# A feed-forward down projection as Strassen block products, seven in place of eight, in a one-core decoder trunk

## The reference, cut to what matters

```python
def swiglu(h, w_gate, w_up, w_down):
    return (jax.nn.silu(h @ w_gate) * (h @ w_up)) @ w_down      # h 256x1024, inner width 2816
# layer 0
x = x + swiglu(rms_norm(x, ffn_norm[j]), ffn_w_gate[j], ffn_w_up[j], ffn_w_down[j])
# layer 1
x = x + pooling_mixer(rms_norm(x, pool_norm[j]), pool_w[j], pool_scale[j])
x = x + moe_swiglu(rms_norm(x, moe_norm[j]), moe_w_router[j], moe_w_gate[j], moe_w_up[j], moe_w_down[j])
```

## Time and profile before

| | us |
|---|---|
| three runs, median (lowest to highest) | 1188.87 (1187.67 to 1188.97) |
| the profiled execution | 1187.06 |
| its span, first to last instruction | 1185.2 |
| TensorE busy in the span | 1155.3 |
| VectorE busy | 190.6 |
| ScalarE busy | 129.3 |
| GpSimd busy | 15.3 |
| bytes moved by DMA | 402.93 MB, mean 340 GB/s |

### The profile page before, as it was taken

One profiled execution on the slowest core, in us unless ns is written; L12 is line 12 of the kernel. 1 busy time (PEld: TensorE's weight loads), 2 busy tenths in 40 slices (PEclk: granted clock), 3 DMA queues, 4 the chain that ended last, 5 costly groups with the idle time before them and its releaser, 6 DMA issues.

```text
span 1185.2 us, 15075 instructions
## 1 busy us (share of the span) xinstructions
PE 1155.3 (97%) x6514; PEld 557.3 (47%) x6515; DVE 190.6 (16%) x382; ACT 129.3 (11%) x280; POOL 15.3 (1%) x52
## 2 busy tenths in 40 slices
PE   8999999999999999999999999999999999999995
PEld 7647888874474342344333335333333533333331
DVE  2642000000042120110121011011101102110102
ACT  1352000010031110000111000011100001010002
POOL 1300000000000000000000000000000000000000
PEclk9999999999999999999999999999999999999998
DMA  8434046536655799999999999999999999999992
GB/s 303 196 123 197 2 176 251 233 140 245 247 232 235 322 402 364 417 431 429 429 431 430 392 429 429 431 431 427 426 433 431 427 430 429 433 427 427 432 430 98
DMA packets 18838, 402.93 MB, mean 340 GB/s; under 512 B 3264, under 2 KB 3264, under 8 KB 4032
## 3 DMA queue, kind: packets, MB, share of 16 engines
q1 hardware_dynamic: 18752, 401.67, 80.7%
HBM read 400.61 MB, written 1.05 MB: 339 GB/s over the span
## 4 chain that ended last, share of the span: by engine, by line
PE 89%; DMA 7%; DVE 2%; ACT 1%; issue 0%; SPq 0%; DVEq 0%; ACTq 0%
PE bank L1321 31%; PE bank L1413 13%; PE bank L1122 13%; PE bank L1302 8%; PE bank L1156 6%; PE bank L1434 4%; DMA ring<-moe_w_up 3%; DMA ring<-moe_w_down 3%; PE bank L1080 2%; PE bank L1024 2%; PE bank L1281 1%; PE bank L1263 1%; PE bank L1000 1%; PE bank L1251 1%; PE bank L1286 1%; PE bank L1379 1%
## 5 line engine op out<-in xcount | busy, mean ns | idle before, releaser
L1321 PE MATMUL bank<-ring,arena 128*64 128x448 f32 x2048 | 391.3, 540 | 1.5 <-DMA ring<-moe_w_up 1.2
L1321 PEld LDWEIGHTS bank<-ring,arena 128*64 128x64 f32 x2048 | 145.1, 137 | 246.6 <-issue 244.6
L1413 PE MATMUL bank<-ring,arena 128*64 128x512 f32 x896 | 199.0, 599 | 6.6 <-DMA ring<-moe_w_down 4.8
L1122 PE MATMUL bank<-ring 128*128 128x256 f32 (+1 forms) x768 | 152.8, 362 | 0.0
L1122 PEld LDWEIGHTS bank<-ring 128*128 128x128 f32 x768 | 136.0, 190 | 17.0 <-issue 0.5
L1413 PEld LDWEIGHTS bank<-ring,arena 128*64 128x64 f32 x896 | 64.2, 138 | 129.8 <-issue 120.4
L1302 PE MATMUL bank<-ring,arena 128*32 128x448 f32 x1024 | 99.7, 541 | 0.0
L1156 PE MATMUL bank<-ring,arena 128*128 128x512 f32 x176 | 75.7, 592 | 0.0
L877 DVE TENSOR_TENSOR arena<-bank,arena 128x448 f32<-128x448 f32 x32 | 20.0, 625 | 334.6 <-PE bank L1321 334.6
L1302 PEld LDWEIGHTS bank<-ring,arena 128*32 128x32 f32 x1024 | 31.5, 110 | 66.6 <-issue 66.6
L1156 PEld LDWEIGHTS bank<-ring,arena 128*128 128x128 f32 x176 | 33.4, 190 | 41.7 <-issue 41.6
(11 more groups left out here) (161 smaller groups left out, 530.3 us busy)
## 6 DMA issues: line engine op xcount, KB each, us to landing
ring<-moe_w_gate SPq DMA_DIRECT2D x32, 3584.0 KB, 22.4
ring<-moe_w_up SPq DMA_DIRECT2D x32, 3584.0 KB, 27.2
ring<-moe_w_down SPq DMA_DIRECT2D x32, 3584.0 KB, 28.0
ring<-ffn_w_gate SPq DMA_DIRECT2D x2, 3072.0 KB, 10.1
ring<-ffn_w_up SPq DMA_DIRECT2D x2, 3072.0 KB, 10.2
ring<-ffn_w_down SPq DMA_DIRECT2D x2, 3072.0 KB, 14.5
ring<-ffn_w_gate SPq DMA_DIRECT2D x2, 2560.0 KB, 13.7
ring<-ffn_w_up SPq DMA_DIRECT2D x2, 2560.0 KB, 19.3
```

What stands on the lines that cost most here:

```text
L1122: last = mm(bank[u % 4][:, half * S + ts.start:half * S + ts.stop], w[:, k, f:f + P], hT[:, k, ts], start=k == 0, stop=k == KD - 1)
L1321: last = mm(bank[2 * (j % 2) + up][64 * h:64 * h + 64, 0:FJ], xg[:, k, side:side + BASE], w[:, k, h, :], start=k == 0, stop=k == KD - 1)
L1413: last = mm(bank[2][64 * h:64 * h + 64, :], hg[:, i0 + i, half * BASE:half * BASE + BASE], w[:, i, h * BANK:h * BANK + BANK], start=d == 0 ...
```

## The change

The 22 tiles are taken as 11 pairs. For a pair (f0, f1) the activations form a 2x2 block matrix (a11 = f0 of token half 0, a21 = f0 of half 1, a12 and a22 the same of f1), the weights another (b11, b12 the column halves of f0, b21, b22 of f1). The four output blocks, before made of eight products, are made of seven (Winograd's form of Strassen): three factors per side that are sums of blocks, s1, s2, s3, s4 and t1 to t4, come from eight additions by VectorE (`combine`), four of 128x512 and four of 128x128; s3 and t3 are written over a21 and b12. Each of the seven products is accumulated over all pairs in its own bank, and the output blocks are put together once at the end. The first eight pairs are streamed, all seven products of a pair in a row; the last three pairs are done product by product, with a11 b11 and a12 b21, which need no sums, first. The sums lie in three buffers that are reused in turn, of which two are in ring buffer 5 and one in `nrm`, and in a fourth where `hT` was. Since ring buffer 5 is in use until the last product, expert chunk 1 is loaded after it, between chunks 2 and 3, and no longer during the feed-forward.

```diff
--- before.py
+++ after.py
@@ -35,6 +35,11 @@
 SLOT = 7168
 FFN_TILES = (6, 6, 5, 5)
 NFT = sum(FFN_TILES)
+PAIRS = NFT // 2
+STREAMED = 8
+PRODUCTS = ("a11 b11", "a12 b21", "s2 t2", "s1 t1", "s4 b22", "s3 t3", "a22 t4")
+PRODUCT_BANK = (4, 5, 2, 3, 0, 6, 7)
+STREAM_ORDER = (0, 1, 5, 6, 2, 3, 4)
 FH = FE // 2
 FJ = FH // 4
 NI = FH // P
@@ -143,6 +148,11 @@
         aT = part(arena, 0, NFT, S)
         silu0 = part(arena, 5632, 2, S)
         band = part(arena, 6144, 4, S + P)
+
+
+        usum = part(arena, 5632, BANK)
+        spare = [part(ring[5], 2048, 1920), part(ring[5], 3968, 1920),
+                 nrm[:, :, :].rearrange("p t d -> p (t d)")[:, 0:1920], part(ring[5], 0, 1920)]
 
 
         poolT = part(arena, 0, KD, S)
@@ -232,7 +242,10 @@
         gu_done = sem("gu_done")
         silu_ready = sem("silu_ready")
         a_ready = sem("a_ready")
-        down0_done = sem("down0_done")
+        comb_ready = sem("comb_ready")
+        pair_done = sem("pair_done")
+        prod_done = sem("prod_done")
+        usum_ready = sem("usum_ready")
         pooled = sem("pooled")
         poolT_ready = sem("poolT_ready")
         router_ready = sem("router_ready")
@@ -317,8 +330,25 @@
         tiles = [sum(FFN_TILES[:j + 1]) for j in range(4)]
         read_by = [(qkv_done, 2), (qkv_done, 4), (qkv_done, 6), (proj_done, 1), (proj_done, 3)]
         read_by += [(gu_done, tiles[j]) for j in range(4) for _ in range(2)]
-        read_by += [(down0_done, 1), (down0_done, 2), (down0_done, 3), (down0_done, 5), (mix_done, 2)]
+        read_by += [(pair_done, 3), (pair_done, 6), (prod_done, 7), (prod_done, 7), (mix_done, 2)]
         assert len(read_by) == C_MOE
+
+        def down_tile(f):
+
+            j = next(i for i in range(4) if f < tiles[i])
+            return C_FFN + 8 + j, stream[C_FFN + 8 + j][0][:, f - tiles[j] + FFN_TILES[j], :]
+
+        def pair_blocks(p):
+
+            f0, f1 = 2 * p, 2 * p + 1
+            w0, w1 = down_tile(f0)[1], down_tile(f1)[1]
+            v = spare[3 if p == STREAMED else p % 3]
+            blk = {"a11": aT[:, f0, 0:P], "a21": aT[:, f0, P:S], "a12": aT[:, f1, 0:P], "a22": aT[:, f1, P:S],
+                   "b11": w0[:, 0:BANK], "b12": w0[:, BANK:D], "b21": w1[:, 0:BANK], "b22": w1[:, BANK:D],
+                   "t1": v[:, 0:BANK], "t2": v[:, BANK:2 * BANK], "t4": v[:, 2 * BANK:3 * BANK],
+                   "s1": v[:, 1536:1664], "s2": v[:, 1664:1792], "s4": v[:, 1792:1920]}
+            blk["s3"], blk["t3"] = blk["a21"], blk["b12"]
+            return blk
 
         def moe_slot(c):
             return MOE_SLOT[c % SLOTS]
@@ -360,16 +390,16 @@
                 if n == C_FFN + 6:
                     sp.wait_ge(x_ready, T)
                     load_chunk(0, 0, 0)
-                if n == C_POOL - 1:
-                    load_chunk(0, 0, 1)
                 if n == C_POOL:
                     sp.dma_start(scale_b, pool_scale[0:1, :].broadcast_to([P, D])).then_inc(full[n % LEAD_SLOTS], 16)
                 sp.dma_start(dst, src).then_inc(full[n % LEAD_SLOTS], 16)
 
             def load_expert(it, e, first=False):
-                for c in range(2 if first else 0, PER_IT):
-
-                    if c >= SLOTS:
+                for c in (2, 1, *range(3, PER_IT)) if first else range(PER_IT):
+
+                    if first and c == 1:
+                        sp.wait_ge(prod_done, 7)
+                    elif c >= SLOTS:
                         b = c - SLOTS
                         sp.wait_ge(up_done if b % 2 else gate_done, 4 * it + b // 2 + 1)
                         sp.wait_ge(upx_done if b % 2 else gatex_done, 4 * it + b // 2 + 1)
@@ -445,7 +475,7 @@
                     own.link(nc.gpsimd.tensor_tensor(b[:, 0:P], b[:, 0:P], ident[:, :], ALU.subtract))
             nc.gpsimd.memset(slot[:, :, NIT:NIT + 1], -1.0).then_inc(band_ready, 1)
 
-            pool.wait_ge(down0_done, 5)
+            pool.wait_ge(prod_done, 7)
             own.step(nc.gpsimd.memset(ones, 1.0))
             own.link(nc.gpsimd.memset(upper, 1.0))
             nc.gpsimd.affine_select(out=upper, in_=upper, compare_op=ALU.is_gt, fill=0.0, base=0,
@@ -535,6 +565,9 @@
                     act.wait_ge(a_ready, u - 1)
                 nc.scalar.activation(silu0[:, u % 2, :], bank[u % 4][:, 0:S], ACT.Silu).then_inc(silu_ready, 1)
             preload(ACT.Sqrt)
+            act.wait_ge(prod_done, 1)
+            act.wait_ge(a_ready, NFT)
+            nc.scalar.activation(usum[:, :], bank[PRODUCT_BANK[0]][:, :], ACT.Copy).then_inc(usum_ready, 1)
             for t in range(T):
                 norm(2, t)
             for t in range(T):
@@ -717,18 +750,48 @@
                 add_x(t, 0, proj_done, t + 2)
                 norm(1, t)
                 keep_hT(t, KD, 4, 2 * T)
+            def combine(p):
+
+
+                b = pair_blocks(p)
+                for f in (2 * p, 2 * p + 1):
+                    n = down_tile(f)[0]
+                    dve.wait_ge(full[ready_at[n][0]], ready_at[n][1])
+                dve.wait_ge(a_ready, 2 * p + 2)
+                if p == STREAMED:
+                    dve.wait_ge(gu_done, NFT)
+                elif p >= 3:
+                    dve.wait_ge(pair_done, p - 2)
+                own.step(nc.vector.tensor_tensor(b["t1"], b["b12"], b["b11"], ALU.subtract))
+                own.link(nc.vector.tensor_tensor(b["s1"], b["a21"], b["a22"], ALU.add))
+                own.step(nc.vector.tensor_tensor(b["t2"], b["b22"], b["t1"], ALU.subtract))
+                own.link(nc.vector.tensor_tensor(b["s2"], b["s1"], b["a11"], ALU.subtract))
+                own.step(nc.vector.tensor_tensor(b["t4"], b["b21"], b["t2"], ALU.subtract))
+                own.step(nc.vector.tensor_tensor(b["s4"], b["a12"], b["s2"], ALU.subtract))
+                own.step(nc.vector.tensor_tensor(b["t3"], b["b22"], b["b12"], ALU.subtract))
+                own.link(nc.vector.tensor_tensor(b["s3"], b["a11"], b["a21"], ALU.subtract))
+                dve.sem_inc(comb_ready, 1)
+
             for u in range(NFT):
                 dve.wait_ge(silu_ready, u + 1)
                 nc.vector.tensor_tensor(aT[:, u, :], bank[u % 4][:, S:2 * S], silu0[:, u % 2, :],
                                         ALU.mult).then_inc(a_ready, 1)
-
-            dve.wait_ge(full[ready_at[C_POOL][0]], ready_at[C_POOL][1])
-            maps = stream[C_POOL][0].rearrange("p (g k) c -> p g k c", k=2)
-            for k in range(2):
-                own.step(nc.vector.tensor_tensor(maps[:, :, k, :], maps[:, :, k, :],
-                                                 scale_b.rearrange("p (g c) -> p g c", g=4), ALU.mult))
-            own.wait()
-            dve.sem_inc(pw_scaled, 1)
+                if u >= NFT - 3:
+                    combine(u - NFT + 3)
+            def scale_maps():
+                dve.wait_ge(full[ready_at[C_POOL][0]], ready_at[C_POOL][1])
+                maps = stream[C_POOL][0].rearrange("p (g k) c -> p g k c", k=2)
+                for k in range(2):
+                    own.step(nc.vector.tensor_tensor(maps[:, :, k, :], maps[:, :, k, :],
+                                                     scale_b.rearrange("p (g c) -> p g c", g=4), ALU.mult))
+                own.wait()
+                dve.sem_inc(pw_scaled, 1)
+
+            for p in range(3, PAIRS):
+                combine(p)
+                if p == STREAMED:
+                    scale_maps()
+
             def keep_poolT(t):
                 for kh in range(2):
                     dve.wait_ge(pooled, 2 * t + kh + 1)
@@ -736,9 +799,32 @@
                            bank[2 * t + kh][:, :].rearrange("p (k s) -> p k s", k=4),
                            2 * KD + 4 * kh, 4).then_inc(poolT_ready, 1)
 
-            add_x(0, 4, down0_done, 4)
+            def product(i):
+                return bank[PRODUCT_BANK[i]][:, :]
+
+            def add_to(dst, src):
+                return nc.vector.tensor_tensor(dst, src, dst, ALU.add)
+
+            xq = [xres[:, t, h * BANK:h * BANK + BANK] for t in range(T) for h in range(2)]
+            dve.wait_ge(usum_ready, 1)
+            own.link(add_to(xq[0], usum))
+            dve.wait_ge(prod_done, 2)
+            own.step(add_to(xq[0], product(1)))
+            dve.wait_ge(prod_done, 3)
+            own.link(add_to(usum, product(2)))
+            own.link(add_to(xq[1], usum))
+            dve.wait_ge(prod_done, 4)
+            own.step(add_to(xq[1], product(3)))
+            own.link(add_to(xq[3], product(3)))
+            dve.wait_ge(prod_done, 5)
+            add_to(xq[1], product(4)).then_inc(x_ready, 1)
             norm(2, 0)
-            add_x(1, 4, down0_done, 5)
+            dve.wait_ge(prod_done, 6)
+            own.link(add_to(usum, product(5)))
+            own.step(add_to(xq[2], usum))
+            own.link(add_to(xq[3], usum))
+            dve.wait_ge(prod_done, 7)
+            add_to(xq[2], product(6)).then_inc(x_ready, 1)
             keep_poolT(0)
             norm(2, 1)
             keep_poolT(1)
```

(38 more changed lines are left out.)

## The result

| | us |
|---|---|
| kernel before, six executions: median (lowest to highest) | 1188.27 (1186.63 to 1189.83) |
| changed kernel, six executions beside them: median (lowest to highest) | 1175.80 (1175.13 to 1178.55) |
| ratio, with 95% interval | 0.9902 (0.9887 to 0.9917) |
| profiled execution of the changed kernel; its span | 1178.55; 1176.6 |
| predicted (range) | 1179.0 (1176.8 to 1183.5) |

Three more series of the same kernel gave 1177.57, 1176.21 and 1178.01, so the first median is the lowest of four.

The account below looks back on a forecast made before the run. TensorE's down-stage instructions were taken to bound the changed stage, with the expert-weight stream as the doubt. Savings of 9.44 + 0.3 = 9.75 us, taken from 1187.06 and 1188.87, gave 1177.3 and 1179.1; predicted 1179.0, range 1176.8 to 1183.5.

Parts of the forecast that it names:

- the price of an instruction: Down stage on TensorE: 0.429 us from start to start, so 22 fewer instructions save 9.44 us.
- The sums: VectorE's additions per pair: 4.0 us, hidden beside TensorE's products; costed at nothing, bounds 0 and 0.9 us.
- x of half 1: End of the down stage: ready about E + 0.8 instead of E + 1.3, E being the stage's end.
- The late chunk: Expert chunk 1 issued after the down stage: two additional chunks, 17.1 us, fit into idle transfer time; cost nothing.
- The sum: Whole kernel: 9.44 us from fewer down-stage instructions plus 0.3 us from putting blocks together, 9.75 us saved.
- theory 1: From the experiments: the change saves the predicted 9.75 us; the rest is which executions caught a half-clock stretch.
- theory 2: From the experiments: a saving the prediction missed; the difference stays at 12 us or more.
- the 0.3 of the sum: After the down stage: TensorE's 0.31 us wait goes as blocks are put together earlier; bounds 0.3 and -0.4.
- VectorE late: Down stage: sums of 6 us or more delay the last group by 4.5 us, giving 1183.5; chance 0.05.
- the chunk is paid: Expert transfers: two chunks more find no idle time, stream ends 7.4 us later, 1196.2; chance 0.05.
- the stream does not yield: Expert weights: bytes own the end, earlier TensorE only waits longer, no change at 1188.9; chance 0.05.
- a smaller price per instruction: Down stage: saving is not 0.429 us each; by weight loads alone 4.2 us, 1184.4; chance 0.05.

Follow-up runs that it names:

- drop: Kernel before with 11 of its 88 down products left out, no sums, no late chunk; 1158.86 us, with tokens routed otherwise.
- add11: Kernel before with 11 more down-stage products into a bank nobody reads, output unchanged; 1198.55 us, ratio 1.0098.
- hold: Changed kernel with the wait for the last pairs' sums moved ahead of the two raw products; 1182.48 us, ratio 0.9953.
- moved: Kernel before with only expert chunk 1 loaded after the last down product, between chunks 2 and 3; 1187.28 us, ratio 0.9998.
- again: Changed kernel run once more, unedited; 1177.57 us, ratio 0.9906.
- again2: Changed kernel run once more, unedited, for the spread; 1176.21 us, ratio 0.9916.
- again3: Changed kernel run once more, unedited, for the number of executions; 1178.01 us, ratio 0.9920.
- steady_after: Changed kernel with ten more products at the start and real products for the router stage's idle-filling transposes; 1176.70 us, ratio 0.9918.
- steady_before: Kernel before with ten more products at the start and real products for the router stage's idle-filling transposes; 1187.90 us, ratio 1.0005.
- twice: Changed kernel with four more VectorE additions of 128x512 in each pair's sums, result unchanged; 1191.54 us, ratio 1.0036.
- late02: Changed kernel with expert chunks 0 and 2 also issued only after the last down product; 1178.04 us, ratio 0.9919.
- all_late: Changed kernel with expert chunks 0 to 5 all issued only when the mixing maps are done; 1189.08 us, ratio 1.0011.

## Why the prediction was wrong, point by point

**What was right.** The direction, the path through the down stage and the price of an instruction. 22 x 0.429 = 9.44 us was measured as 9.46, and the same in `drop` and `add11`. The sums were costed at nothing and cost nothing; a pair takes VectorE 3.54 us where I took 4.0 (my bound below was 3.5). The start of `combine(10)` and what follows, in the changed kernel's timeline of VectorE:

```profile
304.38 0.69 DVE L765 TENSOR_TENSOR ring<-ring 128x512 f32<-128x512 f32 x1 [2.45 <-PE bank L1234]
304.99 0.28 DVE L766 TENSOR_TENSOR ring<-arena 128x128 f32<-128x128 f32 x1
...
307.65 0.28 DVE L772 TENSOR_TENSOR arena<-arena 128x128 f32<-128x128 f32 x1
...
322.38 0.69 DVE L806 TENSOR_TENSOR xres<-bank,xres 128x512 f32<-128x512 f32 x1
```

The single operations are 0.69 and 0.28 us as read off, but starts follow each other sooner than durations add up (0.61 us behind an addition of 512 columns that nobody waits for), which is the missing half microsecond. The last sums end at 307.93, TensorE wants them at 309.23: a cover of 1.3 us, forecast 1.1, and `hold` shows what stands behind it. x of half 1 is ready at 323.07, 0.8 us after the end of the stage, as forecast. pool_w was issued at 274.60 and did not make `scale_maps` wait. The late chunk costs nothing (`moved`), for the reason given: the idle share between the down stage and 392. It landed at 333.65, 11.4 us after the stage (forecast 11), 25 us ahead of its use at 358.93, and the later issues of the SP queue came 8.7 to 8.8 us earlier than before. And the transfers' stretch in the chain starts at 925.02 instead of 933.70: also 8.7 us earlier. Both are the 9.9 us of the change up to the first expert and the 1.5 us by which this trace's down stage started earlier, less the 2.7 us of the router fall.

**The term that was mis-sized: the reference and its spread.** The sum gave 9.75; I set it against 1188.87, the median of three executions, and against a scatter of 1.9 us read from four. Both are too little. The median over 69 executions is 1187.34 (and 1187.23, 1187.34 and 1187.30 in the three later series), so 1.5 us of the miss of 3.2 was there before any change was made: 1187.34 - 9.75 = 1177.6. Another 0.7 us is that the changed kernel's first median, 1175.80, lies below its own over 24 executions, 1176.50; this part is chance. That leaves 1177.6 - 1176.5 = 1.1 us. The lower bound of 1176.8, said to be the low end of the scatter, is not what the rows give: the lowest execution shown leads to 1187.06 - 9.75 = 1177.3. Against the pooled median of the changed kernel it would have missed by 0.3 us.

**The term that was left out: the end of the program.** The sum followed the change to the first expert and took the rest as moved whole. Up to the last work of ScalarE that is so. From the first instruction of L1411 (L1321 before) to there the six traces of the changed kernel, some with edits (its own, `again`, `again2`, `again3`, `steady_after`, `hold`), took 821.3 to 824.1 us, mean 822.95, and the four with all the old products (the kernel before, `moved`, `steady_before`, `add11`) 822.5 to 823.6, mean 823.05. What follows is only the transfer of the second half of the output. The SP queue's wait for it, before and changed:

```profile
SPq L406 <- DMA out<-ring: 2.9, 1, 2.9
```

```profile
SPq L436 <- DMA out<-ring: 2.3, 1, 2.3
```

From issue to landing this transfer takes 3.27, 3.60, 3.62, 3.70 and 3.72 us in the five traces with the old products (the kernel before, `moved`, `steady_before`, `add11`, `drop`), and 2.65 us in each of the nine with the block products. Without `drop` the means differ by 0.9 us. The transfers of the last microseconds, first of the kernel before (1178 to 1186), then of the changed one (1170 to 1177); the last number is the median time to landing of the two output transfers:

```profile
q14 instruction: 1, 0.01, 0.5%
...
out<-ring SPq DMA_DIRECT2D x2, 512.0 KB, 2.9
```

```profile
out<-ring SPq DMA_DIRECT2D x2, 512.0 KB, 2.7
```

In all five traces with the old products one transfer of the queue that the profile calls `instruction` starts 0.9 us after the issue of that output transfer and runs beside it; in none of the nine others does one fall into it (in eight it comes 4.2 to 4.5 us after the issue, when the program has ended, in `twice` the trace has none). That it is what makes the output transfer longer, and why it comes later in the changed program, is not tested. Within the span the sum is then 9.46 + 0.44 + 0.9 = 10.8 us. Device time and span differ by 1.74 us in the mean before and by 1.91 in the changed kernel, which takes 0.17 back: 10.6 us, and all executions together show 10.7 between the means and 10.8 between the medians. So most of what the first series showed above the sum was chance, as theory 1 had it, and about 1 us is a saving that the sum missed, as theory 2 had it, if the other executions are like the traced ones: 0.9 here and 0.14 that the way to the first expert gained beyond the 0.3 of the sum. Less the 0.17, they are 0.9 of the 1.1 us that were left above.

**What the trace of before could have told me.** It carries granted clocks, and I read them only from 333 us on, in the earlier trace rows. Had I read the start, I would have seen the half-clock stretch from 10.4 to 13.6, in a part with nothing but an idle wait ahead of it, and could have asked if it is in every execution. The down stage started at 257.67, 255.92, 256.18, 258.22 and 256.61 us in five traces (before, `moved`, changed, `again`, `hold`), and the way from it to the first expert took 25.1 or 24.7 us without a fall and 25.8 to 28.0 with one. These two places alone move an execution by up to 2.3 and by 1.1 to 2.9 us, whatever the kernel. After the last chunk has landed there is a third: the rest takes 20.2 to 22.4 us in the ten traces of the comparison above, output transfer included, with clock falls in differing places. A range of 2.2 us below the forecast left little room for that.

**What stays open.** Why the transfer of the queue `instruction` comes when it does, and what brings a fall in one execution and not in the next. The waits for experts' chunks in the changed kernel's trace (us, times, longest) are:

```profile
PE bank L1503 <- DMA ring<-moe_w_down: 3.8, 3, 2.3
PE bank L1411 <- DMA ring<-moe_w_up: 1.4, 1, 1.4
```

They sum to 5.2 us; with a router fall they are 4.0 to 4.5 in `again`, `again2` and `again3` and 5.0 and 5.2 in `steady_before` and `moved`, without one 6.4 and 6.7 in `steady_after` and `hold`, 6.0 in the kernel before and 5.6 in `add11`. So a router fall may be partly given back: the experts start later while the transfers go on, and TensorE then waits less for them. That is argued from these sums, not shown by an experiment.

**Chances.** The forecast's mechanism had 0.80 and held, but for the end of the program. Of the rivals, "VectorE late" costs what its rule gives at sums of 6.77 us (`twice`; the 5.5 us from which it should begin was not tried); "the chunk is paid" begins where the idle share is used up (between `late02` and `all_late`); "the stream does not yield" and "a smaller price per instruction" are excluded by `add11`. What was missing was a width, and one term of 0.9 us.

## What to carry to other kernels

Price TensorE work by the distance from start to start and ask of each transfer that is moved whether idle transfer time lies between its new place and the point where the stream is unbroken; both gave the right number here. Compare the two traces to their very last instruction: 0.9 us lay in an output transfer that the change does not touch. Before a range is set, read the granted clock over the whole span, the part that the change does not touch included: a half-clock stretch that could fall otherwise in the next execution belongs into the range, and a median of three executions is itself a measurement with an error. An experiment that leaves work out ahead of a data-dependent branch measures another program: add work that nobody reads instead.

## What the runs showed of the hardware that I had not expected

- Idle time can cost twice. 3.89 us of waiting in `hold` were followed by 12 instructions at 7.09 instead of 5.31 us, 10.89 us in `twice` by 18 instructions at 10.50 instead of 7.89. It need not: 2.96 us in `all_late` were followed by 32 instructions at 6.23 us, the full pace.
- TensorE can be busy without a gap in the records and still fall to half clock: in the router stage of the changed kernel 19.20 of 19.20 us are busy ahead of the fall, and in `again` 6.70 of 6.70 us during it, behind 8-column products and transposes. Of the fourteen traces ten have such a fall in the stage, among them `steady_before` with real products in place of the transposes.
- The fall at the start, about 3.2 us at 0.50 behind 2.3 us of idle time, came in three of fourteen traces, and of the changed kernel, unedited, in one of four. `hold` has the same idle time there, 2.28 us, and no fall.
- The transfer of the last 512 KB of output took 2.65 us in nine traces and 3.27 to 3.72 in the five in which a transfer of the queue `instruction` started 0.9 us after its issue.
